# Attention steps spread over more groups, divides of turned tiles one group later, zero products ahead of the second turn

## What is computed

```
# first block, layer 1: stick-breaking attention, 16 heads of 128
z = q k^T / sqrt(128);  mask = key < query
log_fail = mask ? log_sigmoid(-z) : 0
a = mask ? exp(log_sigmoid(z) + suffix_sum(log_fail) - log_fail) : 0
o = a v;  y = (o * silu(zg)) @ w_out;  h = h + y
# second block
x = rms_norm(h, final_g);  xn = rmsnorm(x);  proj = xn @ w_in
h_m = mlstm(...)                         # 4 heads of 256
h_a = softmax(rope(q) rope(k)^T * sc) v  # 8 heads of 128 (256 tokens: one block, causal)
merged = sigmoid(g_m) * (h_m @ w_m) + sigmoid(g_a) * (h_a @ w_a)
x = x + rmsnorm(merged @ w_out)
x = x + rmsnorm(relu(rmsnorm(x) @ w_up)^2 @ w_down)
```

## Time and profile before

| | |
|---|---|
| Median of 3 runs | 2625.94 us |
| Profiled execution, its own time | 2624.92 us |
| Span of its profile | 2623.1 us |
| TensorE busy | 2594.8 us |
| VectorE busy | 1591.9 us |
| ScalarE busy | 1222.2 us |
| Granted TensorE clock, mean | 0.999 |

### The profile page before, as it was taken

How to read it: one execution, slowest core, us unless ns; L and a number is a source line. 1 busy time by engine, 2 the same in 40 slices (tenths; PEclk the granted TensorE clock), 3 DMA queues, 4 the chain that set the end, 5 groups by cost and what they waited for, 6 DMA issues and landing times.

```text
span 2623.1 us, 29814 instructions
## 1 busy us (share of the span) xinstructions
PE 2594.8 (99%) x11605; PEld 2144.8 (82%) x11605; DVE 1591.9 (61%) x1846; ACT 1222.2 (47%) x1468; POOL 20.9 (1%) x46
## 2 busy tenths in 40 slices
PE   9999999999999999999999999999999999999999
PEld 7888888888887777888888778888878888888887
DVE  5546565566665565766866776555576555565564
ACT  6554443444445455455444444444454344344453
POOL 1000000000000000000000000000000000000000
PEclk9999999999999999999999999999999999999999
DMA  7666666676776766777555777666657676676673
GB/s 259 192 193 204 203 202 195 197 208 200 212 226 187 197 185 193 223 213 221 159 182 172 195 204 216 202 202 195 219 171 225 194 203 215 190 216 206 192 231 128
DMA packets 526205, 526.40 MB, mean 201 GB/s; under 512 B 286432, under 2 KB 289104, under 8 KB 526064
## 3 DMA queue, kind: packets, MB, share of 16 engines
q1 hardware_dynamic: 523536, 517.30, 65.5%
q0 software_dynamic: 2384, 6.93, 1.1%
q10 hardware_dynamic: 144, 0.26, 0.0%
HBM read 488.24 MB, written 2.10 MB: 187 GB/s over the span
## 4 chain that ended last, share of the span: by engine, by line
PE 92%; DVE 3%; DMA 1%; ACT 1%; issue 1%; SPq 1%; DVEq 0%; ACTq 0%
PE bank L33 91%; DVE t_wl L51 1%; SPq L72 1%; DVE t_pool L39 1%; DVE t_pool L51 1%; ACT t_wh L42 0%; PE bank L36 0%; DMA t_xtl<-t_pool 0%; DMA t_vreg<-t_vreg 0%; ACT t_xth L42 0%; DMA t_vreg<-t_pool 0%; DMA t_ytl<-t_pool 0%; DMA t_hres<-in_x_dram 0%; DVE t_hres L51 0%; DVE t_vreg L57 0%
## 5 line engine op out<-in xcount | busy, mean ns | idle before, releaser
L51 DVE TENSOR_TENSOR t_wl<-t_stage,t_wh 128x1024 fp32r<-128x1024 f32 x914 | 1101.4, 1221 | 700.6 <-ACT t_wh L42 698.0
L42 ACT ACTIVATE t_wh<-t_stage 128x1024 fp32r<-128x1024 f32 x914 | 952.2, 1057 | 875.3 <-PE bank L33 845.3
L33 PE MATMUL bank<-t_wl,t_xth 128*128 128x512 f32 x2496 | 980.1, 393 | 9.8 <-DVE t_wl L51 8.5
L33 PE MATMUL bank<-t_wh,t_xth 128*128 128x512 f32 x2496 | 972.4, 390 | 0.0
L33 PE MATMUL bank<-t_wh,t_xtl 128*128 128x512 f32 x2496 | 972.1, 389 | 0.0
L33 PEld LDWEIGHTS bank<-t_wl,t_xth 128*128 128x128 f32 x2496 | 468.9, 188 | 112.3 <-DVE t_wl L51 12.9
L33 PEld LDWEIGHTS bank<-t_wh,t_xtl 128*128 128x128 f32 x2496 | 468.7, 188 | 98.3
L33 PEld LDWEIGHTS bank<-t_wh,t_xth 128*128 128x128 f32 x2496 | 469.5, 188 | 95.7 <-issue 0.2
L33 PE MATMUL bank<-t_wl,t_yth 128*128 128x512 f32 x1024 | 399.2, 390 | 0.0
L33 PE MATMUL bank<-t_wh,t_ytl 128*128 128x512 f32 x1024 | 398.4, 389 | 0.0
L33 PE MATMUL bank<-t_wh,t_yth 128*128 128x512 f32 x1024 | 398.4, 389 | 0.0
(11 more groups left out here) (208 smaller groups left out, 872.9 us busy)
## 6 DMA issues: line engine op xcount, KB each, us to landing
t_stage<-in_a_w_in_dram SPq DMA_DIRECT2D x192, 512.0 KB, 4.3
t_stage<-in_w_in_dram SPq DMA_DIRECT2D x178, 512.0 KB, 4.4
t_stage<-in_b_w_in_dram SPq DMA_DIRECT2D x128, 512.0 KB, 4.4
t_stage<-in_w_up_dram SPq DMA_DIRECT2D x128, 512.0 KB, 4.0
t_stage<-in_w_down_dram SPq DMA_DIRECT2D x128, 512.0 KB, 4.3
t_stage<-in_a_w_out_dram SPq DMA_DIRECT2D x64, 512.0 KB, 4.2
t_ytl<-t_pool SPq DMA_DIRECT2D x128, 128.0 KB, 3.1
t_stage<-in_b_w_out_dram SPq DMA_DIRECT2D x32, 512.0 KB, 5.1
```

Source lines behind the costliest of these rows:

```text
L33: return lambda e: e.matmul(*a, **k)
L42: return lambda e: e.activation(*a, **k)
L51: return lambda e: e.tensor_tensor(*a, **k)
```

## The change

Four things change: (1) in the start, the second turn is issued behind the zero products and not ahead of them; (2) `to_xt` puts three groups between send and divide, not two, and can take pieces that go between; `residual` puts `after` there, with four groups in all for the last chunk; (3) stick-breaking attention does the scan, the Exp with the next scan, and the sends in pieces of their own, two groups for each of the last sends, and starts its score one group later; (4) the second half of a rope gets two groups, and softmax attention takes all row maxima in a piece `highest` ahead of the Exps.

```diff
-        later((send, wait), (divide, 2))
+        later((send, wait), *between, (divide, max(1, gap - len(between))))
...
-    turns[1]()
     busy_matmuls(2)
     pool4_clear = PE.do(lambda e: e.matmul(mbank[1][:, 0:256], blank[:, 0:128], blank, start=True, stop=True))
     temps.free[3] = (pool4_clear,)
+    turns[1]()
     later(*turns[2:])
...
                 to_xt(lambda i, c=c: hres[:, i, cols(c)], (hm,), c, xth, xtl, dest_ready, gain=gain,
-                      done=turned.append)
-                later(lambda c=c, hm=hm, turned=turned: after(c, hm, turned))
+                      done=turned.append, between=(lambda c=c, hm=hm, turned=turned: after(c, hm, turned),),
+                      gap=4 if c == 3 else 3)
...
+        def product(n):
+            u = units[n]
+            u["t"] = AC.do(lambda e: e.activation(u["r"], u["r"], ACT.Exp, scale=-1.0), u["s"])
...
+        def both(*fs):
+            return lambda: [f(n) for f, n in fs]
...
-        return (score, 5), masked, log_fail, step(0), step(1), step(2), step(3), (weigh, 4)
+        return ((score, 6), masked, log_fail, both((tail, 0)), both((product, 0), (tail, 1)),
+                both((product, 1), (tail, 2)), both((product, 2), (send, 0)), (both((send, 1)), 2),
+                (both((send, 2)), 2), (weigh, 4))
...
-        later(lambda: piece(0), lambda: piece(1))
+        later(lambda: piece(0), (lambda: piece(1), 2))
...
+        def highest():
+            for u in units:
+                m = DV.do(lambda e, u=u: e.tensor_reduce(u["mx"], u["ev"], AX, ALU.max), u["m"])
+                u["m"] = DV.do(lambda e, u=u: e.tensor_scalar(u["mx"], u["mx"], -sc, None, ALU.mult), m)
...
-        return ha, ((score, 5), step(0), step(1), step(2), step(3), (weigh, 4))
+        return ha, ((score, 5), highest, both((soften, 0)), both((soften, 1), (send, 0)),
+                    both((soften, 2), (send, 1)), both((send, 2)), (weigh, 4))
```

More of the change, by code:

```diff
@@ L571, in send_turned, with to_xt @@
         return landed
-    def to_xt(src, marks, c, xh, xl, ready, gain=None, scale=1.0, done=None, wait=1):
+    def to_xt(src, marks, c, xh, xl, ready, gain=None, scale=1.0, done=None, wait=1, between=(), gap=3):
         st = {}
@@ L996, in tail @@
             for h in range(u["nh"]):
[L997 to L1000, removed]
+                u["s"] = DV.do(lambda e, h=h: e.tensor_tensor_scan(rev(u["rv"], h, u["nk"]), rev(u["rv"], h, u["nk"]),
+                                                                   rev(u["rv"], h, u["nk"]), 0.0, ALU.add, ALU.bypass),
+                               u["l"])
+        def product(n):
+            u = units[n]
+            u["t"] = AC.do(lambda e: e.activation(u["r"], u["r"], ACT.Exp, scale=-1.0), u["s"])
         def send(n):
@@ L1494, in score @@
                 scored.append(mm)
+        def highest():
+            for u in units:
+                m = DV.do(lambda e, u=u: e.tensor_reduce(u["mx"], u["ev"], AX, ALU.max), u["m"])
+                u["m"] = DV.do(lambda e, u=u: e.tensor_scalar(u["mx"], u["mx"], -sc, None, ALU.mult), m)
         def soften(n):
             u = units[n]
-            m = DV.do(lambda e: e.tensor_reduce(u["mx"], u["ev"], AX, ALU.max), u["m"])
-            m = DV.do(lambda e: e.tensor_scalar(u["mx"], u["mx"], -sc, None, ALU.mult), m)
             for h in range(u["nh"]):
@@ L1502, in soften @@
                                                            bias=u["mx"][:, h:h + 1], scale=sc,
-                                                           accum_out=u["sm"][:, h:h + 1]), m)
+                                                           accum_out=u["sm"][:, h:h + 1]), u["m"])
         def send(n):
```

## The result

The changed kernel takes 2598.25 us, the median of 4 runs (2597.51 to 2598.6), against 2626.03 for the kernel before in 4 runs of the same chip (2625.48 to 2626.22): a ratio of 0.9894 [0.9877, 0.9911], the brackets being the 95% interval. The profiled execution took 2598.6 us, its span is 2596.9.

What follows compares the result with a forecast made beforehand. TensorE's product stream was taken as the bound, with only its gaps to win. Terms 12.6 + 1.8 + 0.8 + 5.4 + 2.7 = 23.3 us gave 2602.6 on the median's footing, stated as 2602.5; range 2599 to 2611.

Steps and rivals of the forecast that it cites:

- What bounds the kernel: Whole kernel: TensorE, busy 2594.8 of 2623.1 us, is the bound; only gaps in its product stream can be won.
- Stick-breaking: Stick-breaking attention, four chunks: separating scan, Exp and send removes the late-half wait (6.8 us) and weigh wait (5.8): 12.6 us.
- No low half comes more than 4 us after: Stick-breaking attention: in the new order low halves come at most 4 us after their earliest time, against 10.9 of slack.
- Rival (d): Stick-breaking attention: the five weight-half slots are the bound, so 6.8 us stay, 2609 us; chance 0.07.
- Divides: Divide behind squares and scale in the last residual gains 1.8 us; a group later elsewhere, at the first up projection, 0.8.
- rival (f): Eleven hand-overs: the divide comes too late, a missed group at each costs 30 us, so 2632 us; chance 0.04.
- Softmax attention: Rope and softmax attention: less blocking by the divide and two groups for rope's second half gain 5.4 us.
- rival (b): Softmax attention: rope itself keeps VectorE behind, ScalarE's block is the smaller cause; 5.4 us stay, 2608 us; chance 0.12.
- Start: Start: zero products ahead of the second turn fill its wait, gaining 1.4 us, plus 1.3 if the clock stays up: 2.7.
- rival (a): Start: the clock falls all the same, costing 1.3 us, 2603.8 us; chance 0.12.
- (c): Stick-breaking weigh step: the weigh's turned tile still lands late; 5.8 us stay, 2608 us; chance 0.08.
- (e): Whole kernel: waits only move, later steps piling onto the next projections; all but the start stays, 2623 us; chance 0.07.

Runs made afterwards that it cites:

- scan ahead: Kernel before with each stick-breaking scan one group ahead of its Exp, sends one group each, score as before: 2611.1 us, 0.9948.
- two other orders: Kernel before with only stick-breaking scans a group ahead of their Exps, 2611.1 us; or only sends moved behind and spread, score a group later, 2613.51 us.
- the whole: The changed kernel with all edits; at half the slack, weight halves made two groups ahead in place of four: 2625.89 us, period 70.61.
- The two old starts of 5.30 us: Traces of both kernels with stick-breaking scans ahead of their Exps and the start unchanged: 5.30 us from second turn to second weight group.
- the repeat: The changed kernel unaltered, run again: 2598.46 us against 2625.32 for the kernel before, 0.9897, 26.9 us less.
- the old order and 3 groups ahead: Kernel before with weight halves made three groups ahead in place of four, five slots kept: 2647.21 us.
- the stick-breaking order alone: Kernel before with only the stick-breaking edit (scan, Exp and send in separate groups, score one group later): 2611.68 us, 0.9952.

## Why the prediction came out as it did

**What bounds the kernel** was right: with TensorE's gaps closed it is 100% busy, and nearly all of the gain lies at waits that have a row.

**Stick-breaking.** Right in mechanism. Both waits went, the weigh wait because lateness had made it: it goes with scan ahead too, where each send keeps one group. "No low half comes more than 4 us after" was 10.9 - 6.0 = 4.9. Rival (d), that another order changes nothing with five slots, is out: two other orders closed the gap with the same five, and the whole keeps its period at half the slack. The rule of the Trainium skill (Perfetto Trace Analysis, Optimization Strategy) is that a repeated gap can mean too little room. The traces bear it out in part: a high half waits 1.25 us for its slot in each chunk of the old order, and with that wait gone 1.3 us came back. A sixth slot might thus have closed much of the gap without another order, which no run shows: more than five were not tried.

**Divides.** The mechanism was right in the residual and the up projection; rival (f) did not come. At the tightest hand-over I counted on, the last residual, the tile is ready 0.4 us ahead of its group (0.5 to 1.0 forecast). Worth 2.2 with the old attention and 3.8 with the new, which I did not foresee.

**Softmax attention.** The gain came, its cause was half told. I put the divide's block against rope (rival (b)) as if one had to be the larger; either alone would have given most of it. Rival (b)'s time could not come out for that reason.

**Start.** Right to 0.1 us against this trace of before, the clock too; rival (a) did not come. That it is so close is partly luck, as the start of the kernel before differs from execution to execution. The two old starts of 5.30 us, which have no slow stretch, put the order at 0.8 to 1.0 (1.4 forecast), and so the slow products in the trace of before at some 1.6 (1.3 forecast). Rivals (c) and (e) are refuted by the waits after.

**What failed is the size of a wait.** The step was "I add 0.25 to a wait between wide products, 0.15 to one between narrow ones". In the three heads of the earlier trace rows 16 waits went and 17.3 us of rows; my terms outside the start made 20.6 of them, and those parts won 23.7. From start to start, product by product, the 16 cost 22.2: on the mean 0.31 each beyond the row. Low halves took 0.26 to 0.32, near the 0.25 of the step; the turned tiles, counted as narrow, took 0.28 in stick-breaking and 0.39 in softmax attention in place of 0.15. The reason is that rows show only part of a wait: a product's modelled time is 0.39 us and the pitch 0.23, so the first 0.16 us are covered, and the next pitches lose some 0.15 more.

The other 1.5 us were not in the sum at all. One is a wait of 0.18 for a turned tile in the last residual, which cost 0.43. The rest, 1.1, has no row, because a wait shorter than what is covered leaves hardly any. In softmax attention before, TensorE:

```profile
1467.01 0.39 PE L33 MATMUL bank<-t_wh,t_xtl 128*128 128x512 f32 x1
1467.33 0.50 PE L33 MATMUL bank<-t_wl,t_xth 128*128 128x512 f32 x1
...
1469.99 0.39 PE L33 MATMUL bank<-t_wh,t_xtl 128*128 128x512 f32 x1
1470.42 0.50 PE L33 MATMUL bank<-t_wl,t_xth 128*128 128x512 f32 x1
```

Starts 0.32 and 0.43 apart and a first product of 0.50: two restarts, no bracket. Low halves ended 0.05 and 0.06 us ahead of them. Three such groups make 1.1 of the 1.7 by which the softmax term is short; stick-breaking is short by 0.9, all of it at waits that have rows, the residual by 0.4. The low end of the range had only the small waits that have rows.

With the sizes as measured the sum on the median's footing is 2625.94 - 26.3 = 2599.6, inside the range. The other 1.4 us are single executions of the kernel before, which ranged over 5.3 us in 21 runs; the repeat gave 26.9.

## What to carry to other kernels

Measure the spare time of each prepared operand up to its first use, and compare the sum of delays with the slack: when two delays meet one slack, removing either removes the wait, the second removal wins only margin, and the gains of parts don't add. Take the cost of waits from start to start of the stream's instructions, not from idle rows, and expect a wait that grows to swallow the one behind it. For a kernel that scatters by 5 us, a gain of 2 or 3 is read from lined-up traces rather than from a few medians.

## What the runs showed of the hardware

The same wait does not always cost the same clock. With the old order and 3 groups ahead, each chunk has the 2.75 us wait shown above. Windows of the first chunk and then the second (columns as in the earlier trace rows):

```profile
815.00:817.00 2.00, 1.21 (x5) 1.03 (x6) 1.97 (x3) 2.00 (x3) 0.00 (x0) 1.00 0.32 56
...
888.00:890.00 2.00, 0.23 (x1) 0.23 (x2) 1.51 (x2) 2.00 (x3) 0.00 (x0) 0.86 0.51 84
890.00:892.00 2.00, 2.00 (x5) 1.59 (x6) 1.97 (x3) 2.00 (x3) 0.00 (x0) 0.50 0.53 131
892.00:894.00 2.00, 2.00 (x8) 1.59 (x7) 2.00 (x3) 0.24 (x1) 0.00 (x0) 0.79 0.74 200
```

In the second to fourth chunk the clock falls to 0.50, that is 1.2 GHz, and products start 0.43 us apart until it is back by 894; in the first it stays at 1.00 behind a wait of the same length. That is the 1.2 us between their periods. In the kernel before, the wait of 1.45 us is followed by 1.00 in all four chunks. Why it fell in three chunks of four was not settled.

The recorded clock is not the whole of the pace. TensorE at the start, with the stick-breaking order alone and then with scan ahead alone, both with the old start:

```profile
6.73 1.09 PE L36 MATMUL bank<-t_ident,t_hres 128*128 128x128 f32 x4 [1.26 <-DMA t_hres<-in_x_dram]
7.61 2.49 PE L33 MATMUL bank<-t_pool 128*128 128x256 f32 x6
```

```profile
6.94 0.63 PE L36 MATMUL bank<-t_ident,t_hres 128*128 128x128 f32 x4 [1.83 <-DVE t_xtl L54]
7.40 1.46 PE L33 MATMUL bank<-t_pool 128*128 128x256 f32 x6
```

The recorded clock is 1.00 from 5 to 13 us in both. From the turn to the second weight group the first takes 6.73 us, near the 6.93 to 6.99 of the four traces that show 0.50, the second 5.30; two others, at a recorded 1.00 as well, take 7.62 and 7.72. Why was not settled.
